# Thirty-two experts: the gather with the one-hot as the stationary side, and the dense path placed behind the end

## The reference, cut to what matters

```python
logits = xt @ w_router + b_router                  # 256 tokens, 32 experts
top_val, top_idx = lax.top_k(logits, 4)
gates = jax.nn.softmax(top_val, axis=-1)
# every expert e gets the tokens that chose it:
hdn = xb @ w_up[e] + b_up[e]                       # 1024 -> 2048
gate_h = jnp.minimum(hdn[:, :1024], 7.0)
up_h = jnp.clip(hdn[:, 1024:], -7.0, 7.0)
act = (up_h + 1.0) * gate_h * jax.nn.sigmoid(1.702 * gate_h)
y = act @ w_down[e] + b_down[e]                    # 1024 -> 1024
out = out.at[slot_token].add(y * gate)
```

## Time and profile before

| | us |
|---|---|
| runs | 2530.53, 2526.93, 2531.21 (median 2530.53) |
| the profiled execution's own time | 2527.22 |
| its span, first to last instruction | 2525.3 |
| PE busy | 2380.2 (94%) |
| DVE busy | 594.1 (24%) |
| ACT busy | 521.0 (21%) |
| from expert 0's first matmul to the last scatter | 1491 to 2470 |

### The profile page before, as it was taken

How to read it: one execution, slowest core, us unless ns; L and a number is a source line. 1 busy time by engine, 2 the same in 40 slices (tenths; PEclk the granted TensorE clock), 3 DMA queues, 4 the chain that set the end, 5 groups by cost and what they waited for, 6 DMA issues and landing times.

```text
span 2525.3 us, 35082 instructions
## 1 busy us (share of the span) xinstructions
PE 2380.2 (94%) x15260; PEld 1842.6 (73%) x15260; DVE 594.1 (24%) x1694; ACT 521.0 (21%) x1223; POOL 45.8 (2%) x64
## 2 busy tenths in 40 slices
PE   6988999999999889999999989999999999999997
PEld 3676788888887567887778864677666677666666
DVE  2044410000005421001675321122222222222223
ACT  3244432210003333200534120011111111111112
POOL 0000200000000000000000000000000000000000
PEclk9999999999999999999999979999999999999998
DMA  8811211123313514435333546899999999999990
GB/s 347 325 67 55 113 67 67 67 95 138 134 67 134 200 67 167 156 144 192 137 134 122 221 177 260 337 426 426 427 426 427 426 427 426 428 425 427 427 398 27
DMA packets 42123, 601.71 MB, mean 238 GB/s; under 512 B 4673, under 2 KB 5185, under 8 KB 5601
## 3 DMA queue, kind: packets, MB, share of 16 engines
q1 hardware_dynamic: 41472, 593.30, 57.6%
q10 hardware_dynamic: 480, 5.97, 0.6%
HBM read 598.20 MB, written 1.05 MB: 237 GB/s over the span
## 4 chain that ended last, share of the span: by engine, by line
PE 91%; DVE 4%; DMA 2%; ACT 1%; issue 1%; POOL 0%; DVEq 0%; SPq 0%; POOLq 0%; ACTq 0%
PE PS L906 19%; PE PS L559 13%; PE PS L550 13%; PE PS L931 9%; PE PS L692 7%; PE PS L879 5%; PE PS L441 3%; PE PS L540 3%; PE PS L943 3%; DMA RG<-in_w_ada 2%; PE PS L901 2%; PE PS L497 1%; PE PS L1030 1%; PE PS L397 1%; PE PS L382 1%
## 5 line engine op out<-in xcount | busy, mean ns | idle before, releaser
L550 PE MATMUL PS<-HN,RG 128*128 128x256 f32 x1536 | 333.9, 380 | 4.0 <-ACT HN L1108 4.0
L559 PE MATMUL PS<-BIG,RG 128*128 128x256 f32 x1536 | 333.1, 379 | 0.0
L550 PEld LDWEIGHTS PS<-HN,RG 128*128 128x128 f32 x1536 | 292.8, 191 | 44.6 <-issue 4.6
L559 PEld LDWEIGHTS PS<-BIG,RG 128*128 128x128 f32 x1536 | 291.4, 190 | 42.8 <-issue 3.4
L906 PE MATMUL PS<-BIG,XS 128*64 128x256 f32 (+1 forms) x2016 | 234.9, 384 | 0.0
L1063 ACT ACTIVATE BIG<-PS 128x256 f32<-128x256 f32 (+1 forms) x247 | 102.5, 422 | 519.6 <-PE PS L550 243.7
L906 PEld LDWEIGHTS PS<-BIG,XS 128*64 128x64 f32 (+1 forms) x2016 | 145.7, 138 | 87.0 <-issue 19.9
L1947 DVE TENSOR_SCALAR STAT<-PS 128x128 f32<-128x128 f32 (+1 forms) x128 | 37.8, 296 | 648.0 <-PE PS L906 648.0
L906 PE MATMUL PS<-RG,XS 128*64 128x256 f32 (+1 forms) x1520 | 180.0, 388 | 0.0
L692 PE MATMUL PS<-XS,RG 128*128 128x256 f32 x768 | 172.1, 382 | 5.0 <-DVE XS L1570 4.1
L692 PEld LDWEIGHTS PS<-XS,RG 128*128 128x128 f32 x768 | 145.7, 192 | 26.6 <-issue 6.9
(11 more groups left out here) (285 smaller groups left out, 2350.5 us busy)
## 6 DMA issues: line engine op xcount, KB each, us to landing
BIG<-in_w_up SPq DMA_DIRECT2D x64, 2048.0 KB, 16.4
RG<-in_w_up SPq DMA_DIRECT2D x48, 2048.0 KB, 15.9
RG<-in_w_ff SPq DMA_DIRECT2D x32, 2048.0 KB, 8.0
BIG<-in_w_down SPq DMA_DIRECT2D x32, 2048.0 KB, 18.0
RG<-in_w_ada SPq DMA_DIRECT2D x24, 2048.0 KB, 8.7
RG<-in_w_down SPq DMA_DIRECT2D x24, 2048.0 KB, 19.5
RG<-in_w_in SPq DMA_DIRECT2D x23, 2048.0 KB, 7.8
SM<-in_w_up SPq DMA_DIRECT2D x16, 2048.0 KB, 16.5
```

The lines of the kernel that those rows point to most:

```text
L550: m = pe.matmul(banks[b][:, 0:256], w[:, k, 128 * n:128 * n + 128], own(HN, s)[:, k, :], start=k == 0, stop=k == 7)
L559: m = pe.matmul(banks[b][:, 0:256], w[:, k, :], own(FFH, s)[:, k, :], start=k == 0, stop=k == 31)
```

## The change

The gather is turned round. SEL's first 64 slots (64 columns) are now the stationary side and HTM the moving one, with 512 features at a time. The two halves of the features go to partitions 0 to 63 and 64 to 127 of one bank (`picked`, 4 matmuls). ACT copies the bank to XT, a new view of 512 columns; 4 transposes set it upright again (`upright`), and ACT copies that into XG. The transposes of the activations are split around the gather: the first half stands ahead of it, the second half and the transposes of SELG behind it, then the upright transposes, which wait for ACT's first copy.

Only 64 of an expert's 128 slots are gathered ahead. A broad expert picks its upper 64 at the start of its own body: `picked` with the other half of SEL, a copy by VectorE, `upright`, and another copy by VectorE, all ahead of its up chunks.

The dense path moves on PE, ACT and DVE from between the experts and the end part to behind everything else, reached by a branch. What is computed stays the same. The name of the change also speaks of sums of squares on GpSimd: nothing of them differs between the two programs.

```diff
@@ -313,6 +313,7 @@
         AV = CAT_[:, 0:1024]
         AVT = CAT_[:, 1024:2048]
         YV = CAT_[:, 2048:3072]
+        XT = CAT_[:, 2560:3072]
         SEL = CAT_[:, 3072:3328].rearrange("p (a s) -> p a s", a=2)
         SELG = CAT_[:, 3328:3584].rearrange("p (a s) -> p a s", a=2)
         SCT = STAT[:, 1280:1536]
...
@@ -869,16 +870,37 @@
                 pe.wait_ge(s_landed[s], 16 * nth)
                 return ring(s).rearrange("p (k n) -> p k n", k=8)
+            def picked(b, part):
+                for tt in range(2):
+                    for half in range(2):
+                        m = pe.matmul(banks[b][64 * half:64 * half + 64, :], SEL[:, tt, 64 * part:64 * part + 64],
+                                      HTM[:, tt, 512 * half:512 * half + 512], start=tt == 0, stop=tt == 1)
+                return m
+            def upright(b):
+                for i in range(4):
+                    m = pe.transpose(banks[b][:, 128 * i:128 * i + 128], XT[:, 128 * i:128 * i + 128], ID2)
+                return m
             def gather(ex):
                 pe.wait_ge(s_sel, ex + 1)
-                for half in range(2):
-                    b = take(("xg", ex, half))
-                    for kk in range(4):
-                        k = 4 * half + kk
-                        for tt in range(2):
-                            m = pe.matmul(banks[b][:, kk * 128:kk * 128 + 128], HTM[:, tt, k * 128:k * 128 + 128], SEL[:, tt, :],
-                                          start=tt == 0, stop=tt == 1)
-                    m.then_inc(s_full[b], 1)
+                b = take(("xt", ex))
+                picked(b, 0).then_inc(s_full[b], 1)
+            def gather_turn(ex):
+                read_out(("xt", ex))
+                b = take(("xg", ex))
+                upright(b).then_inc(s_full[b], 1)
+            def activated(ex, half, wd):
+                b = take(("at", ex, half))
+                pe.wait_ge(s_av, 4 * ex + 2 * half + 2)
+                for i in range(wd // 128):
+                    c, hh = (2 * half + i // 2, i % 2) if wd == 512 else (2 * half + i, 0)
+                    m = pe.transpose(banks[b][:, i * 128:i * 128 + 128], AV[:, c * 256 + hh * 128:c * 256 + hh * 128 + 128], ID2)
+                m.then_inc(s_full[b], 1)
             def half_of(b, h, sides):
@@ -889,8 +911,15 @@
                 cap = 128 if broad else 64
                 sides = 1 if broad else 2
                 wd = 512 if broad else 256
-                read_out(("xg", ex, 0))
-                read_out(("xg", ex, 1))
+                read_out(("xg", ex))
+                if broad:
+                    b = F.pool[F.turn % 4]
+                    pe.wait_ge(s_free[b], F.n[b])
+                    pe.wait_ge(s_selg, ex + 1)
+                    picked(b, 1).then_inc(s_more, 1)
+                    pe.wait_ge(s_mcopy, 2 * ex + 1)
+                    upright(b).then_inc(s_more, 1)
+                    pe.wait_ge(s_mcopy, 2 * ex + 2)
                 for c in range(4):
                     if c % 2 == 0:
                         for q in c, c + 1:
@@ -904,21 +933,20 @@
                     for k in range(8):
                         for h in range(sides):
                             i = pe.matmul(half_of(b, h, sides), Xg[:, k, 0:cap], w[:, k, h * wd:h * wd + wd], start=False, stop=k == 7)
+                            if not broad and c == h == 0 and k < 2:
+                                i.then_inc(s_more, 1)
                     i.then_inc(s_used, 1)
+                activated(ex, 0, wd)
                 if ex + 1 < NEXP:
                     gather(ex + 1)
-                for half in range(2):
-                    b = take(("at", ex, half))
-                    pe.wait_ge(s_av, 4 * ex + 2 * half + 2)
-                    for i in range(wd // 128):
-                        c, hh = (2 * half + i // 2, i % 2) if broad else (2 * half + i, 0)
-                        m = pe.transpose(banks[b][:, i * 128:i * 128 + 128], AV[:, c * 256 + hh * 128:c * 256 + hh * 128 + 128], ID2)
-                    m.then_inc(s_full[b], 1)
+                activated(ex, 1, wd)
                 b = take(("sc", ex))
                 pe.wait_ge(s_selg, ex + 1)
                 for tt in range(2):
                     m = pe.transpose(banks[b][:, tt * 128:tt * 128 + 128], SELG[:, tt, :], ID2)
                 m.then_inc(s_full[b], 1)
+                if ex + 1 < NEXP:
+                    gather_turn(ex + 1)
                 T_ = AVT[:, 0:8 * cap].rearrange("p (k s) -> p k s", k=8)
                 for c in range(2):
                     w = expert_chunk(ex, 4 + c)
@@ -977,11 +1005,14 @@
                                           stop=ex == NEXP - 1 and k == 7, skip_group_check=True)
                     m.then_inc(s_used, 1)
-            with pe.If_cmp(over, 0, "IS_EQ"):
+            fork = nc.cur_bb
+            pe.br_cmp(over, 0, on_true="pe_sparse", on_false="pe_dense", comp_op="IS_EQ")
+            with nc.body("pe_sparse", valid_engines=[mybir.EngineType.PE]):
                 for tt in range(2):
                     for half in range(2):
                         read_out(("ht", tt, half))
                 gather(0)
+                gather_turn(0)
                 ahead = []
                 for ex in range(NEXP):
                     ahead.append((F.state(), nc.cur_bb))
@@ -992,11 +1023,8 @@
                     nc.switch_bb(f"pe_next{ex}")
                 pe.wait_ge(s_scat, NEXP)
                 pe.sem_inc(s_join, 1)
-            with pe.Else():
-                for ex in range(NEXP):
-                    dense(ex)
-                pe.wait_ge(s_used, 6 * NEXP)
-                pe.sem_inc(s_join, 1)
+                pe.br("pe_end")
+            nc.switch_bb("pe_end")
             pe.wait_ge(s_join, 3)
@@ -1038,6 +1066,15 @@
                 with nc.body(f"pe_broad{ex}", parent=at, valid_engines=[mybir.EngineType.PE]):
                     expert(ex, True)
                     pe.br(f"pe_next{ex}")
+            with nc.body("pe_dense", parent=fork, valid_engines=[mybir.EngineType.PE]):
+                for ex in range(NEXP):
+                    dense(ex)
+                pe.wait_ge(s_used, 6 * NEXP)
+                pe.sem_inc(s_join, 1)
+                pe.br("pe_end")
         @block.scalar
         def _(act):
...
@@ -1426,8 +1463,10 @@
             act.load(over, FLAG[0:1, 32:33])
             def gathered(ex):
-                for half in range(2):
-                    evac(XG[ex % 2][:, 4 * half:4 * half + 4, :].rearrange("p k s -> p (k s)"), ("xg", ex, half), part=slice(0, 512))
+                evac(XT, ("xt", ex), part=slice(0, 512))
+                b = full(("xg", ex))
+                act.activation(XG[ex % 2][:, :, 0:64].rearrange("p (h i) s -> p h i s", h=2),
+                               banks[b][:, :].rearrange("p (i h s) -> p h i s", i=4, h=2), ACT.Copy).then_inc(s_free[b], 1)
             def expert(ex, broad):
                 sides = 2 if broad else 1
...
@@ -1922,9 +1969,10 @@
             def select(ex):
                 if ex:
-                    full(("xg", ex - 1, 1))
+                    full(("xt", ex - 1))
                 for tt in range(2):
-                    i = dve.tensor_scalar(SEL[:, tt, :], IOTA, POS[:, tt, ex:ex + 1], MSK[:, tt, ex:ex + 1], ALU.is_equal, ALU.mult)
+                    i = dve.tensor_scalar(SEL[:, tt, 0:64], IOTA[:, 0:64], POS[:, tt, ex:ex + 1], MSK[:, tt, ex:ex + 1],
+                                          ALU.is_equal, ALU.mult)
                 i.then_inc(s_sel, 1)
             def expert(ex, broad):
@@ -1932,10 +1980,23 @@
                 wd = 512 if broad else 256
                 if ex:
                     full(("sc", ex - 1))
+                if broad:
+                    for tt in range(2):
+                        dve.tensor_scalar(SEL[:, tt, 64:128], IOTA[:, 64:128], POS[:, tt, ex:ex + 1], MSK[:, tt, ex:ex + 1],
+                                          ALU.is_equal, ALU.mult)
                 for tt in range(2):
                     i = dve.tensor_scalar(SELG[:, tt, :], IOTA if broad else IOTA2, POS[:, tt, ex:ex + 1], GTE[:, tt, ex:ex + 1],
                                           ALU.is_equal, ALU.mult)
+                    if not broad and tt == 0:
+                        i.then_inc(s_mcopy, 2)
                 i.then_inc(s_selg, 1)
+                if broad:
+                    b = F.at["up", ex, 0][0]
+                    dve.wait_ge(s_more, 2 * ex + 1)
+                    dve.tensor_copy(XT, banks[b][:, :]).then_inc(s_mcopy, 1)
+                    dve.wait_ge(s_more, 2 * ex + 2)
+                    dve.tensor_copy(XG[ex % 2][:, :, 64:128].rearrange("p (h i) s -> p h i s", h=2),
+                                    banks[b][:, :].rearrange("p (i h s) -> p h i s", i=4, h=2)).then_inc(s_mcopy, 1)
                 if ex + 1 < NEXP:
                     select(ex + 1)
                 for c in range(4):
@@ -1983,7 +2044,9 @@
                         dve.wait_ge(s_used, 6 * ex)
```

(25 more changed lines are left out.)

13 lines of the change are left out of this document (7 added, 6 removed).

## The result

The changed kernel takes 2516.45 us (median of 5 runs, 2514.24 to 2519.32), the one before 2530.53 (2526.93 to 2534.23). The ratio is 0.9948, with a 95% interval of 0.9933 to 0.9962: faster by 13 us. Forecast were 2517 and a gain of 12.6.

The account below looks back on a forecast made before the run. Weight transfers (29.78 us per expert) were taken as already slower than TensorE (29.27), hidden by the ring. Span 2525.3 - 10.0 (last chunk) - 2.6 (exit) = 2512.7 us; run median forecast 2517, range 2509 to 2528.

Parts of the forecast that it names:

- Narrow expert, -1.65: From up to down chunks of a narrow expert: TensorE needs 3.36 us instead of 5.00, 1.65 us less.
- Start of the stream, -0.7: Up to the first slot freed behind the broad expert: savings and the added pick sum to 0.7 us earlier.
- upper pick: Start of the broad expert's body: picking its upper 64 slots adds 4.1 us, bounds 3.3 and 6.3.
- Gather 0: Gather ahead of the first expert, at a low clock: 5.1 us instead of 6.45, so 1.4 us saved.
- Pace of the stream, -1.4: The 171 chunks up to the last: small holes closing give 0.5 us, fewer instruction blocks 0.9 us.
- Last chunk, -10.0: End of the expert stage: TensorE starts the last chunk near 2454.5 us instead of 2464.53, soon after its landing.
- Exit, -2.6: From last scatter to VectorE's first sum: 0.5 us instead of 3.1 with the dense code moved away, saving 2.6.
- One: New gather's two halves stream one behind the other, 3.5 us instead of 1.78: 2538 us, slower; chance 5%.
- Two: TensorE, waiting for chunks in the expert stage, loses its clock once per expert: 2529 us, no change; chance 7%.
- Three: In unprofiled runs the transfers already bind the expert stage: 2526 us, within no change; chance 10%.
- Four: Weight transfers can go faster when asked earlier, so the narrow experts' 50 us count: 2479 us; chance 3%.
- What would show it: Signs expected in the new profile, such as gather near 1.8 us, 0.8 us idle behind ACT, clock 1.00.

Follow-up runs that it names:

- e4: Changed kernel with only half of each w_down chunk transferred, all TensorE instructions kept; ratio to the kernel before 0.9816.
- e1: Changed kernel with the dense path put back between the experts and the end part, new gather kept; ratio to the kernel before 0.9984.
- e10: Changed kernel, unaltered, measured and profiled a second time; ratio to the kernel before 0.9938.
- e2: Kernel before with only the dense path moved behind everything, old gather kept; ratio to the kernel before 0.9980.
- e3: Kernel before with only half of each w_down chunk transferred, all TensorE instructions kept; ratio to the kernel before 0.9994.
- e8: Changed kernel with GpSimd stepping an unused semaphore 64 times after each of the 192 chunks; span 2558.8 us, a single run.

## Why the prediction was right, and where it was not

The total was right (12.6 us forecast, 13 in the runs), and so was the mechanism: TensorE is faster than the weights, the ring's reserve is used up, and of 40 us which the gather is worth (e4) 6 to 10 arrive. That the total came so close was in part luck: in the first profile two errors of size cancel, since I had put the gain at the last chunk 3.7 us too high and that at the exit 3.4 too low. From g to the end the first profile is 12.3 us shorter than the one before, the second 15.8.

- *Narrow expert, -1.65.* Measured -1.40 (27.87 us). The chain from up to down chunks was 0.23 us longer than forecast: 0.15 in the first transposes (0.37 for 0.22) and 0.16 in the upright ones (0.59 for 0.43), while the gather with its copy was 0.08 shorter (2.63 for 2.71). It did not matter, since the transfers bind.
- *Start of the stream, -0.7.* Here the size failed. From g to expert 2 it is +4.7 in the profile after, +4.2 in e1, +1.3 in e10 and e4. My 4.1 us for the upper pick assumed TensorE at full clock; it ran at 0.50 and took 6.4 us, which was my upper bound (5.7 in e10, where the clock was low for part of it). The first pair of the broad expert's chunks behind it lost another 0.7 us to the clock. The jump ahead of it cost 5.87 us here, against 4.72 before, and I had written that it stays; over all profiles it took 4.66 to 5.87 us with either gather, so this part is scatter. Gather 0 gave 0.7 instead of 1.4: its eight records took 3.68 us at a clock of 0.50, where I had 2.65.
- *Pace of the stream, -1.4.* Measured 847.9 against 850.2 us, -2.3. The time of the 171 chunks was priced well, their cause by guess, and the guess is not borne out: over 20 experts in the middle the pace is the same in both kernels (595.1 us). What was gained lies at the two ends of the stream.
- *Last chunk, -10.0.* Measured -6.3 in the first profile, -6.6 in e1 and -9.9 in e10. The miss in the first profile is that of the stream's start. TensorE starts the chunk 0.04 us after its landing, as said.
- *Exit, -2.6.* Measured -6.0 in the profile after, -4.6 by e2. The stall itself went from 3.13 to 0.15 us, so -3.0. The term left out was the clock: behind the stall TensorE worked at a low clock, and its first 16 records now take 1.7 us less. The rest varies between profiles. The Trainium skill, "Runtime: NRT & Kernel Launch", section Instruction fetch mechanics, has a taken branch stall when its target lies outside the two pages of code at hand. The trace agrees: 3.13 us with the dense path to cross, 0.15 without.
- *Rivals.* One fell on L877's 1.86 us. Two fell, but not without a trace: TensorE waits in pieces of at most 2.6 us and mostly near 1, and the clock fell once, behind the longest, for 1.7 us. I had named a clock under 1.00 in the stage as a sign of being wrong; the sign came, at a size that changed nothing. The Trainium skill, "TensorE: Matmul & The Clock Gate", section HAM oscillation, tells of a kernel whose wait for each tile is longer than the tile's matmuls, and which starts every tile at the low clock. Here the waits are shorter than a chunk's 3.67 us of matmuls, and the trace shows the fall once in 740 us. Three fell in e3. Four fell on the 4.89 us that remained, with e4 to show what it would have brought.
- *What would show it.* The marks came but for three, the clock among them. TensorE was not idle for 0.8 us behind ACT's copy, since transposes fill that time. And I had the transfers bind from about expert 10; they do from 15, and only from there does TensorE wait for DMA. The time to landing had 22.9 us to grow, from 12.5 us at expert 3's last chunk to 35.4, and grew by 29.7 - 27.87 = 1.8 us per expert: 12 experts. Even my own 2.2 us per expert would have made it number 13.

## What to carry to other kernels

A stage that shows TensorE and the transfers both near full needs one more view before anything in it is made faster: the time to landing of single transfers, early and late in the stage. If it grows, the ring is being used up, and the reserve at the end (here 8 us) is the gain to expect, not the instructions saved. Once transfers bind, what counts is what comes before their stream begins, and a stall can cost more than its length, since the work behind it may start at a low clock (here 1.7 us on top of 3.0).

## What I had not expected of the hardware

- A stall ahead of the end part cost more in TensorE's clock: 16 records took 5.38 us behind idle times of 4.17 and 3.86 us (before, e3) and 6.34 behind 5.96 (e1), instead of 3.69. Once 2.58 us of waiting were enough: 32 records in 5.36 us instead of 3.67.
- GpSimd running 6144 memsets of 128x1 back to back (202 us) held a VectorE tensor_scalar on SBUF for 199 us, though it waits for nothing of GpSimd's. The Trainium skill, "SBUF — State Buffer", section Who interferes with whom, has the port pair that the two share locked for a whole instruction when VectorE's works in a 2-port mode, which it lists as possible for tensor_scalar. Here the wait lasted over all 6144 of GpSimd's; whether it was for the port is not shown.
- 12288 additional instructions on GpSimd, 86 blocks of 8 KB on their queue while the weights streamed, delayed a saturated stream by 49 us, 0.57 us per block, while their bytes are 0.2% of the traffic (one run).
- The same code ahead of the experts led to a start of expert 0's gather anywhere from 1490.0 us (e8) to 1504.4 (e1), over nine profiles in which nothing ahead of it was altered. Whether chip, build or execution makes the difference was not tried.
